# First jobs of a two-layer streaming encoder one by one, the next layer's first slab in its own place, partial sums on VectorE, the root table ahead of time, cache copies in mid attention

## The reference, cut to what matters

```python
def _layer(x, pos, cache, ...):
    z = x @ w_in                          # [q_A | k_A | v_A | c_q | c_kv | k_rope]
    q = einsum(_rms_norm(cq, q_norm), w_uq)        # squares of c_q are summed over 384 features
    ckv = _rms_norm(ckv, kv_norm); kr = _rope(kr, pos)
    y_a = banded sink attention (window 128, T5 bias);  y_b = latent attention
    g = jax.nn.sigmoid(x @ w_gate + b_gate)
    h = g[..., :D_MODEL] * (y_a @ w_proj_a) + g[..., D_MODEL:] * (y_b @ w_proj_b)
    x = _layer_norm(ALPHA * x + h @ w_out, ln1_g, ln1_b)
    f, conv_state = _conv_ffn(x, conv_hist, w_up, conv_w, conv_b, w_down)
    x = _layer_norm(ALPHA * x + f, ln2_g, ln2_b)
    return x, (win_k, win_v, ckv, kr, conv_state)   # window = the last 128 rows: kept cache rows + 16 new ones
```

## Time and profile before

| | us |
|---|---|
| three runs | 1922.37, 1924.11, 1924.13 (median 1924.11) |
| profiled execution | 1922.85, of which the recorded span is 1921.1 |
| granted TensorE clock, mean | 0.993 |
| busy in the span | PE 1865.4, DVE 1009.3, ACT 659.7, POOL 544.4 |
| DMA | 169.44 MB, 88 GB/s on the mean |

### The profile page before, as it was taken

How to read it: one execution, slowest core, us unless ns; L and a number is a source line. 1 busy time by engine, 2 the same in 40 slices (tenths; PEclk the granted TensorE clock), 3 DMA queues, 4 the chain that set the end, 5 groups by cost and what they waited for, 6 DMA issues and landing times.

```text
span 1921.1 us, 32071 instructions
## 1 busy us (share of the span) xinstructions
PE 1865.4 (97%) x12562; PEld 1770.5 (92%) x12562; DVE 1009.3 (53%) x1584; ACT 659.7 (34%) x1388; POOL 544.4 (28%) x241
## 2 busy tenths in 40 slices
PE   7998999999999999999999999999999999999996
PEld 6987888899999999999998888879999999999995
DVE  3466544458854423443674665444597443334447
ACT  3245333432433212332332453334343332133323
POOL 2321111133143334332322311111322332433231
PEclk9999999999999999999999999999999999999998
DMA  6442232232122122111241523223221221222121
GB/s 180 120 144 76 94 105 86 104 121 88 45 88 82 50 88 88 66 70 55 83 137 42 158 69 106 96 74 133 94 82 69 72 74 66 77 88 73 55 73 55
DMA packets 58802, 169.44 MB, mean 88 GB/s; under 512 B 8120, under 2 KB 26216, under 8 KB 50728
## 3 DMA queue, kind: packets, MB, share of 16 engines
q1 hardware_dynamic: 58696, 167.97, 26.3%
HBM read 149.42 MB, written 18.28 MB: 87 GB/s over the span
## 4 chain that ended last, share of the span: by engine, by line
PE 91%; DVE 5%; DMA 2%; POOL 1%; issue 1%; ACT 1%; SPq 0%; ACTq 0%; DVEq 0%; POOLq 0%
PE ps L1514 61%; PE ps L1759 10%; PE ps L1839 3%; PE ps L1548 3%; PE ps L1693 2%; PE ps L1665 2%; PE ps L1561 2%; PE ps L1736 1%; DMA gate_logits<-logits 1%; DVE res L1329 1%; DVE res L1325 1%; PE ps L1672 1%; PE ps L1674 1%; POOL w_lo L648 1%; PE ps L1740 1%; PE ps L1522 1%
## 5 line engine op out<-in xcount | busy, mean ns | idle before, releaser
L648 POOL TENSOR_TENSOR w_lo<-w_raw,w_hi 128x1024 fp32r<-128x1024 f32 (+2 forms) x237 | 544.1, 2304 | 1340.8 <-ACT w_hi L712 1329.8
L712 ACT ACTIVATE w_hi<-w_raw 128x1024 fp32r<-128x1024 f32 (+2 forms) x236 | 225.4, 974 | 465.6 <-PE ps L1514 441.7
L1514 PE MATMUL ps<-x_hi,w_hi 128*128 128x320 f32 x1408 | 321.4, 309 | 0.0
L1514 PE MATMUL ps<-x_lo,w_hi 128*128 128x320 f32 x1408 | 321.0, 309 | 0.0
L1514 PE MATMUL ps<-x_hi,w_lo 128*128 128x320 f32 x1408 | 320.6, 309 | 0.0
L1514 PEld LDWEIGHTS ps<-x_hi,w_lo 128*128 128x128 f32 x1408 | 235.5, 188 | 0.0
L1514 PEld LDWEIGHTS ps<-x_hi,w_hi 128*128 128x128 f32 x1408 | 235.2, 188 | 0.3
L1514 PEld LDWEIGHTS ps<-x_lo,w_hi 128*128 128x128 f32 x1408 | 235.3, 188 | 0.0
L1759 PE MATMUL ps<-x_hi,w_hi 128*128 128x320 f32 x512 | 164.9, 322 | 7.1 <-ACT logits L800 7.1
L1414 DVE TENSOR_SCALAR f_conv<-f_ext,vec 128x656 f32<-128x656 f32 x44 | 64.6, 1469 | 201.8 <-ACT tail L934 199.3
L1759 PE MATMUL ps<-x_hi,w_lo 128*128 128x320 f32 x512 | 159.5, 311 | 0.0
(11 more groups left out here) (255 smaller groups left out, 3206.4 us busy)
## 6 DMA issues: line engine op xcount, KB each, us to landing
w_raw<-in_slabs SPq DMA_DIRECT2D x86, 1024.0 KB, 4.8
w_raw<-in_slabs SPq DMA_DIRECT2D x20, 768.0 KB, 4.0
gate_logits<-logits SPq DMA_DIRECT2D x64, 160.0 KB, 1.9
gates<-gate_logits SPq DMA_DIRECT2D x16, 640.0 KB, 6.2
w_raw<-in_slabs SPq DMA_DIRECT2D x16, 640.0 KB, 3.7
ckvc<-in_ckvc SPq DMA_DIRECT2D x16, 256.0 KB, 2.7
ckvc_t<-in_ckvc_t SPq DMA_DIRECT2D x16, 256.0 KB, 2.9
x_in<-in_x_t SPq DMA_DIRECT2D x4, 640.0 KB, 9.0
```

Source lines behind the costliest of these rows:

```text
L648: pool.tensor_tensor(w_lo[:, s % 2, c], w_raw[:, s % 2, c], w_hi[:, s % 2, c].bitcast(F32), ALU.subtract).then_inc(wlo_ready, 1)
L712: A(w_hi[:, s % 2, c], w_raw[:, s % 2, c], ACT.Copy).then_inc(whi_ready, 1)
L1514: ins = MM(out_[:, a, :], w, x[:, t, a * HT:(a + 1) * HT], start=t == 0 and w is wh and x is hi, stop=t == tiles - 1 and w is wl)
```

## The change

Seven edits:

1. **Start.** SP loads slabs 0 and 1 by halves, the first half slab ahead of all x, the second half of x last. ACT copies in that order. DVE subtracts the first half slab itself, POOL the other three. TensorE's first pass runs job by job (`start`): hi x hi and hi x lo over the 8 tiles, then lo x hi, and only then the next job, which needs the next half slab.
2. **Squares of c_q.** DVE adds the three tiles of squares (two adds of 128 x 640, `sq_added`), and TensorE sums one tile where it summed three (J_SCQ: two matmuls for six).
3. **Kept cache rows.** The two copies move from before the first gate store to the middle of attention's gate stores.
4. **First half of the norms.** DVE adds the eighth tile too (`add_last`), and TensorE's sum of the first half is one matmul where it was two, for the sums and for the squares. The second half stays.
5. **Root table.** ACT takes a root of one element just before the last jobs of each norm (`root_table`).
6. **Next layer's first slab.** Slab NS gets its own place (`first_hi`, `first_lo`, in space that is free there); ACT copies it before the last squares and POOL subtracts it from there. Slab NS+1 goes to slot 0 once the last job but one of the down projection is done. Layer 1's `four` reads both from there.
7. Counters follow (`low_count`).

```diff
@@ SP, start
-            for k in range(4):
+            def load_x(k):
                 a, t = k // 2, slice(k % 2 * 4, k % 2 * 4 + 4)
                 sp.dma_start(x_in[:, t, cols(a)], inp["x_t"][:, t, cols(a)]).then_inc(x_loaded[k], 16)
-                if k < 2:
-                    sp.dma_start(w_raw[:, k, 0:SLAB_W[k]], inp["slabs"][k, :, 0:SLAB_W[k]]).then_inc(raw_loaded[k], 16)
+            def load_half(s, half):
+                c = half_slab(s, half)
+                sp.dma_start(w_raw[:, s, c], inp["slabs"][s, :, c]).then_inc((raw_loaded if half else first_raw)[s], 16)
+            load_half(0, 0)
+            load_x(0)
+            load_x(1)
+            load_half(0, 1)
+            load_half(1, 0)
+            load_half(1, 1)
+            load_x(2)
+            load_x(3)
@@ SP, attention
                 load_gate(3)
-                sp.dma_start(out["kc_keep"]...
-                sp.dma_start(out["vc_keep"]...
...
                     if c % 4 == 3:
                         store_gate(c // 4)
+                    if c == 4 * NG // 2:
+                        sp.dma_start(out["kc_keep"]...
+                        sp.dma_start(out["vc_keep"]...
@@ POOL
-            low(0, 0)
+            low(0, 0, made=1, other=0)
             low(1, 1)
...
-                    low(NS, NS, layer)
-                    low(NS + 1, NS + 1, layer, low_count(layer, 1) - 2)
+                    low(NS, NS, layer, at=(first_hi, first_lo))
+                    low(NS + 1, NS + 1, layer, low_count(layer, 1) - 2, slot=0)
@@ ACT
+            first_high(0, 0)
+            for k in range(KD):
+                first_x(0, k)
+            first_high(0, 1)
+            first_high(1, 0)
+            first_high(1, 1)
+            for k in range(KD):
+                first_x(1, k)
...
-                    act.wait_ge(added_sq_h[a], base + 1)
+                    act.wait_ge(added_sq_h[a], base * 2 + 2 if a == 0 else base + 1)
...
+                root_table()
                 shift(J_DN2)
...
-                    norm(1, J_DN2, V_B2, lambda: high(NS), lambda: high(NS + 1), (third_z[0], NS + 2))
+                    third_high(first_hi, NS, layer * (NS * 8) + 8 * NS + 16)
+                    def second_high():
+                        act.wait_ge(raw_loaded[1], layer * (NS * 8) + 8 * NS + 16)
+                        act.wait_ge(job_done, layer * NJ + JC + before_norm(J_DN2, KF) + 1)
+                        for half in range(2):
+                            c = half_slab(NS + 1, half)
+                            A(w_hi[:, 0, c], w_raw[:, 1, c], ACT.Copy).then_inc(whi_ready, 1)
+                    norm(1, J_DN2, V_B2, second_high, lambda: None, (third_z[0], NS + 2))
@@ DVE
+            weights_low(w_lo[:, 0, :], w_hi[:, 0, :], 0, 0, 1)
+            for a in range(2):
+                for k in range(KD):
+                    first_low(a, k)
...
+                for k in range(KQ - 1):
+                    dve.wait_ge(sq_ready, layer * (KQ + 1) + KQ)
...
+                    TT(cq_sq[:, KQ - 1, :], cq_sq[:, KQ - 1, :], cq_sq[:, k, :], ALU.add).then_inc(sq_added, 1)
                 dve.wait_ge(par_loaded, layer * (16 * N_PAR) + 16 * (N_PAR - 2))
...
+                def add_last(which):
+                    base, c = layer * 2 + which, cols(0)
...
+                    TT(sum_d[:, c], sum_d[:, c], res[:, KD - 1, c], ALU.add).then_inc(added_d_h[0], 1)
...
+                    TT(sum_sq[:, c], sum_sq[:, c], sq[:, 1, c], ALU.add).then_inc(added_sq_h[0], 1)
...
                     last_sum_half(which, n7, 0, KF + 1)
                     add_sq_half(which, 0)
+                    add_last(which)
                     last_sum_half(which, n6, 1, KF)
@@ PE
+                def start():
+                    for j in range(4):
+                        weights(j // 2, j % 2)
+                        c0 = j % 2 * KD
+                        for t in range(KD):
+                            pe.wait_ge(xn_hi[0], t + 1)
+                            c = (c0 + t) * P
+                            for k, w in enumerate((w_hi, w_lo)):
+                                MM(one(j, 0), w[:, j // 2, c:c + P], x_hi[:, t, cols(0)], start=t == 0 and k == 0, stop=False)
+                        for t in range(KD):
+                            pe.wait_ge(xn_lo[0], t + 1)
+                            c = (c0 + t) * P
+                            MM(one(j, 0), w_hi[:, j // 2, c:c + P], x_lo[:, t, cols(0)], start=False, stop=t == KD - 1)
...
-                    for k in tiles:
-                        ins = full(n, ones[:], cq_sq[:, k, :], k == tiles[0], k == tiles[-1])
-                    ins.then_inc(job_done, 1)
+                    if n == J_SCQ:
+                        pe.wait_ge(sq_added, layer * (KQ - 1) + KQ - 1)
+                    full(n, ones[:], cq_sq[:, k, :]).then_inc(job_done, 1)
...
                         if a == 0:
                             start_job(n)
+                            pe.wait_ge(added, base * 2 + 2)
+                            MM(one(n, a), ones[:], rest[:, cols(a)], start=True, stop=True).then_inc(first_half_done, 1)
+                            continue
```

More of the change, by code:

```diff
@@ L111, in low_count @@
 def low_count(layer, which):
-    return 2 + 3 * (2 * layer + which + 1) if layer >= 0 else 2
+    return 3 + 3 * (2 * layer + which + 1) if layer >= 0 else 3
 def half_slab(s, half):
@@ L1523, in full, with four, part @@
                     return ins
-                def four(n, s, before):
+                def start():
[11 more added lines that the diff above has]
+                            MM(one(j, 0), w_hi[:, j // 2, c:c + P], x_lo[:, t, cols(0)], start=False, stop=t == KD - 1)
+                def four(n, s, before, first=False, at=None):
+                    at = [(w_hi[:, k, :], [w_lo[:, k, 0:1024], w_lo[:, k, 1024:2048]]) for k in range(2)] if at is None else at
+                    def part(j, t, low):
+                        hi, lows = at[j // 2]
+                        return lows[j % 2][:, t * P:(t + 1) * P] if low else hi[:, (j % 2 * KD + t) * P:(j % 2 * KD + t + 1) * P]
                     for a in range(2):
+                        if first and a == 0:
+                            start()
+                            continue
                         if a == 1:
@@ L1545, in four @@
                                         weights(s + slot, j % 2)
-                                c = (j % 2 * KD + t) * P
-                                for k, w in enumerate((w_hi,) if late else (w_hi, w_lo)):
-                                    MM(one(n + j, a), w[:, slot, c:c + P], x_hi[:, t, cols(a)],
+                                for k in range(1 if late else 2):
+                                    MM(one(n + j, a), part(j, t, k), x_hi[:, t, cols(a)],
                                        start=t == 0 and k == 0, stop=False)
@@ L1568, in z @@
                     dense(n, s, tile0, KD, x_hi, x_lo, part, at=at)
-                four(0, 0, layer * (2 * KD))
+                if layer == 0:
+                    four(0, 0, 0, first=True)
+                else:
+                    four(0, 0, layer * (2 * KD), at=[(first_hi, first_lo), (w_hi[:, 0, :], [w_lo[:, 0, 0:1024], w_lo[:, 0, 1024:2048]])])
                 z(4, 2, 0, 2, third_z)
```

77 lines of the change are left out of this document (44 added, 33 removed).

## The result

The changed kernel takes 1906.03 us (median of four runs, 1905.65 to 1906.51) where the kernel before takes 1923.72 on the same chip; the ratio is 0.9907, 95% interval 0.9896 to 0.9919. So 17.7 us are won, 3 less than the 20.65 of the sum, inside the stated range.

A forecast was written before the change was run, and what follows sets the result against it. TensorE was taken as the bound, working 1865.4 of 1921.1 us. Terms sum to 20.65 us: 1902.2 from the profiled 1922.85, 1903.5 from the median; stated 1903.0, range 1896.5 to 1911.5.

The forecast's parts named there:

- Copies: Start of attention: moving the kept cache rows' copies shortens TensorE's waits for `logits`; 4.7 and 4.4, together 9.1 us.
- Between the layers: Layer boundary: early copy and subtraction of slab NS end the `x_lo` matmuls at 971.9 instead of 977.7; 5.8 us.
- rival 3: Between the layers: GpSimd's two subtractions hold DVE's sums and TensorE waits some 3 us; 1906 us, chance 0.07.
- Squares of c_q in layer 1: Layer 1's squares' sums: TensorE waits nowhere around them, so the records that go are won; 2.15 us.
- End: Last norm: loses the same 1.07 us of TensorE sums; 1.0 us won, ends 0.5 and 1.1.
- First norms: LayerNorm 1, both layers: two TensorE sums go, 0.45 us won twice; 0.9 us, ends 0 and 2.1.
- Head of layer 0: Start through job 12: the chain of loads binds, so the earlier start gains only 1.7 us, ends 0.7 and 3.3.
- rival 1: Head of layer 0: the loads don't bind it, so the time is 1895 us; chance 0.07.
- the head moves only as far as `vec` does: Layer 0: loads issued in order from `vec` set jobs 9 and 12; `vec` moves 1.4 us, plus 0.3 slack.
- Rival 4: Layer 0's projections: the new wait before job 9 leaves matmuls long at lower clock, slower than before; chance 0.02.
- the forecast's own 1899 to 1907: Whole kernel: narrower range in us from the ends of the head, the boundary and the norms; chance 0.72.
- a wait of 4 to 5 us at job 9: Expected profile sign in layer 0: TensorE's new wait, put to slab 4 or its subtraction.

The follow-up runs named there:

- run 6: Changed kernel with the two copies of the kept cache rows back ahead of the first gate stores; 1914.68 us.
- run 7: Changed kernel with the next layer's first slab back in its usual place, copied only after the root; 1913.36 us.
- run 8: Changed kernel with TensorE again summing the eighth tile of the norms' first half (`add_last` left out); 1911.13 us.
- run 10: Changed kernel without the early roots, so the root table is loaded between sums and root of each norm; 1907.42 us.
- run 1: Changed kernel with only its start undone: slabs 0 and 1 whole, x before them, first four jobs together; 1908.44 us.
- run 4: Changed kernel with four matmuls that serve nothing added in layer 0 between job 11 and job 12; 1904.59 us.
- run 12: Changed kernel unaltered, profiled a second time on one chip with the kernel before; 1906.45 us, one run.
- run 2: Changed kernel with parameters up to `hist`, slab 4 and slab 5 issued ahead of the masks' and bias table's write; 1902.64 us.

## Why the prediction was right, and where it was not

- **Copies** (9.1): right, 4.59 + 4.24; the wait fell to 0.63 in both layers, the clock stayed, and run 6 brought both losses back. In mid attention they are free: the cache rows behind them are issued from 244.35 and land up to 4.7 us after their issue, the scores that read them start at 254.84.
- **Between the layers** (5.8): right, 5.91. Carrying the pattern of the first norm over worked because it was the same sequence of steps; undoing the slab's place alone loses 5.7 (run 7), the sums alone 1.10 (run 8), the early root alone 0.41 (run 10), more than the whole gain together, so here too they overlap. Of rival 3 the first half came and the second did not: GpSimd holds two of DVE's sums to 2.61 and 2.68 us (run 7 shows them), but it is done at 944.20, before the forecast 945.5, and DVE has 0.81 us to spare, so TensorE does not wait.
- **Squares of c_q in layer 1** (2.15): 2.15. **End** (1.0): 1.05. **First norms** (0.9): 1.5, of which run 10 shows 1.46 to hang on the early root, which the sum had not priced by itself, and run 8 0.8 on the sums. The two are not independent, so their costs don't add up to the gain.
- **Head of layer 0** (1.7): wrong in sign. The first half held: `vec` moved by 1.16 (forecast 1.4), the first pass won 7.2 us, and the loads, not the first jobs, set the end, against rival 1. The step that failed is "the head moves only as far as `vec` does". It assumed that the chain behind `vec` takes the same time. Of the 1.16 us, 0.50 were lost between `vec` and the issue of the table's write, the write took 1.83 more (34.72 against 32.89), and slab 5 landed 0.29 later behind it: 1.46 later in all and not 1.4 earlier, and job 12, which had 0.3 of slack, started 1.17 later. Against run 1, whose write is as long, job 12 does come earlier, by 0.77 (87.44 against 88.21), so the start moves the chain as forecast, if by less; what the sum had wrong is that the rest of the change leaves the chain alone. Why the write is longer stays open.
- **The waits in the head** are the other part of this miss. I let TensorE run from job 9 to job 12 without a wait and gave 0.3 us of slack, but a TensorE that is early everywhere waits wherever the chain binds, in three places (1.83, 3.02, 2.19), and behind the last the clock cost 1.57 us that nothing gave back in these profiles (nothing of it in run 10's). Rival 4 named this mechanism, for job 9; there it cost 2.6 us (16.90 from job 9 to job 11, 14.32 in the kernel before) and changed nothing, since job 12 waited anyway.
- The **range** held, and so did the forecast's own 1899 to 1907, near its upper end: the head's miss of 4.4 us was no larger than the room left for the other terms, which all came as forecast. For the head that is luck, not working: its own ends (0.7 to 3.3) did not contain -2.74. They had no end below nothing, though no row excluded a loss.
- Forecast signs seen: first matmul 8.12 (8.4), `vec` 22.48 (22.2), a wait of 4 to 5 us at job 9 (1.83 + 3.02, in two places), 8 records at the squares' sums, no table load in front of the root, no wait for `x_hi` between the layers.

## What to carry to other kernels

When a stage is bound by a chain of loads, work that is done earlier in front of it is not neutral: it turns into waits, and behind a wait TensorE may run at half its clock (0.50 to 0.57 behind the waits of 3.02 and 2.19 us, 1.00 behind run 10's 2.41); price the clock at the **last** of these waits, the one from which nothing is given back. Before moving early work forward, look at what is issued ahead of the loads that bind: here one slow write stood in front of loads that did not need it, and taking them past it, together with two roots past a copy, was worth 11.7 us, two thirds of the whole change. When several edits meet in one chain (sums and root), undo each alone: each can be worth more than its share of the gain.

## What the runs showed of the hardware that was not expected

- Four matmuls that serve nothing, put into a wait, went with a kernel 1.4 us faster in the median (run 4), the clock behind the wait being 1.00 where it was 0.57. Behind an unfilled wait of 2.41 us it was 1.00 too (run 10), behind others of 2.14 to 3.65 us it fell.
- The same wait for `krc_t`, 0.3 to 0.9 us, was followed by a lower clock and 3.2 us lost in two profiles (waits of 0.84 and 0.85 us, runs 7 and 8) and by none in another with a wait of 0.88 us (run 12). Its length alone doesn't tell it. The second runs of these two kernels were 3.1 and 3.7 us faster than the profiled ones, which would fit a fall that comes in one execution and not in the next; those runs have no profile.
- While the table is written, the DMA engines are busy to 0.46 and move 55 GB/s (32 to 56 us), and each small load that SP issues in that time takes it 3.9 to 4.6 us to issue, the first 6.6; ahead of the write one takes 0.43 (`hist` 4.36 behind the write's issue in the changed kernel, 0.43 ahead of it in run 2).
